# Modulation chunks in the order 0, 2, 1, 3, with z's products in halves between them

## What is computed

```python
mod   = silu(c) @ w_ada + b_ada        # sh1, sc1, g1, sh2, sc2, g2: six rows of 1024
mod_c = silu(c_ctx) @ w_ada + b_ada
u  = (rms_norm(x,   norm_pre_mix) * (1 + sc1)  + sh1)  @ w_in    # latent tokens
uc = (rms_norm(ctx, norm_pre_mix) * (1 + csc1) + csh1) @ w_in    # context tokens
# u is split: q, k, v and gate z of the delta rule, xs, B, C and gate z of the state space part,
# 48 small columns. Convolutions, two scans in both directions, w_out and a norm follow,
# then the mixture of experts: 32 experts, top 4, and the last norm
```

## Time and profile before

| | us |
|---|---|
| device time, median of 3 runs | 1446.82 |
| lowest and highest | 1443.19, 1450.98 |
| span of the profiled execution (its own device time isn't recorded apart) | 1447.1 |
| TensorE busy (matmul) in that span | 1279.4 |
| VectorE, ScalarE, GpSimd busy | 479.3, 253.1, 123.0 |
| first z product starts | 40.09 |
| last small product ends | 82.56 |

### The profile page before, as it was taken

The page is one execution under the profiler, slowest core; times in us unless marked ns, Lnnn a source line. Parts: engine busy times, 40 slices in busy tenths (PEclk is TensorE's granted clock), DMA queues, the critical chain, the costliest instruction groups (busy, mean ns, idle before and its releaser), DMA issues.

```text
span 1447.1 us, 26834 instructions
## 1 busy us (share of the span) xinstructions
PE 1279.4 (88%) x11016; PEld 586.6 (41%) x11017; DVE 479.3 (33%) x1023; ACT 253.1 (17%) x492; POOL 123.0 (8%) x168
## 2 busy tenths in 40 slices
PE   5999899447897999989898889887998999999995
PEld 1556444346665334333333333332433433433432
DVE  1236346742586423223221222121322322322323
ACT  2321523023514111111111111100100100100101
POOL 0201413443411000000000000000000000000000
PEclk9999999656798999999999999999999999999998
DMA  9506273010057799999999999999999699969993
GB/s 362 238 30 226 80 252 140 2 33 5 23 208 269 304 427 428 429 428 428 428 428 428 428 428 428 427 427 427 427 428 428 260 428 428 428 279 415 428 428 149
DMA packets 47822, 458.85 MB, mean 317 GB/s; under 512 B 4369, under 2 KB 4753, under 8 KB 22673
## 3 DMA queue, kind: packets, MB, share of 16 engines
q1 hardware_dynamic: 47762, 457.96, 76.3%
HBM read 456.31 MB, written 1.05 MB: 316 GB/s over the span
## 4 chain that ended last, share of the span: by engine, by line
PE 41%; DMA 28%; DVE 2%; ACT 1%; issue 1%; DVEq 0%; ACTq 0%
DMA arena<-in_w_up 28%; PE bank L1138 21%; PE bank L1167 8%; PE bank L1109 3%; PE bank L1100 2%; PE bank L1031 2%; PE bank L870 1%; ACT arena L1521 1%; PE bank L1131 1%; PE bank L1162 1%; ACT arena L1519 0%; PE bank L974 0%; PE bank L986 0%; PE bank L996 0%; PE bank L1042 0%
## 5 line engine op out<-in xcount | busy, mean ns | idle before, releaser
L1138 PE MATMUL bank<-arena 128*64 128x512 f32 x2176 | 483.1, 597 | 34.1 <-DMA arena<-in_w_up 19.7
L1138 PEld LDWEIGHTS bank<-arena 128*64 128x64 f32 x2176 | 154.1, 137 | 344.3 <-issue 269.6
L1167 PE MATMUL bank<-arena 128*64 128x512 f32 x1088 | 239.4, 592 | 0.0
L2179 DVE TENSOR_SCALAR arena<-bank 128x512 f32<-128x512 f32 x34 | 23.6, 693 | 390.9 <-PE bank L1138 390.9
L1167 PEld LDWEIGHTS bank<-arena 128*64 128x64 f32 x1088 | 78.2, 136 | 138.4 <-issue 136.0
L638 PE MATMUL bank<-arena 128*128 128x512 f32 (+1 forms) x320 | 122.4, 539 | 0.6 <-DMA arena<-in_wfm 0.6
L2160 DVE TENSOR_TENSOR arena<-arena,bank 128x512 f32<-128x512 f32 x140 | 86.6, 682 | 6.0 <-PE bank L1109 6.0
L638 PEld LDWEIGHTS bank<-arena 128*128 128x128 f32 x320 | 60.5, 192 | 60.5 <-issue 54.9
L1100 PEld LDWEIGHTS bank<-arena 128*128 128x128 bf16 x1680 | 60.4, 119 | 27.0 <-DVE arena L2183 25.8
L1109 PE MATMUL bank<-arena 64*128 64x512 f32 x280 | 69.6, 614 | 0.9 <-ACT arena L1523 0.9
L1100 PE MATMUL bank<-arena 128*128 128x64 bf16 x1680 | 64.2, 199 | 1.1 <-DVE arena L2101 1.1
(11 more groups left out here) (339 smaller groups left out, 1107.1 us busy)
## 6 DMA issues: line engine op xcount, KB each, us to landing
arena<-in_w_gate SPq DMA_DIRECT2D x64, 2048.0 KB, 20.1
arena<-in_w_up SPq DMA_DIRECT2D x64, 2048.0 KB, 21.7
arena<-in_w_down SPq DMA_DIRECT2D x64, 2048.0 KB, 20.3
arena<-in_w_ada SPq DMA_DIRECT2D x12, 2048.0 KB, 8.9
arena<-in_wfm SPq DMA_DIRECT2D x20, 512.0 KB, 6.6
arena<-in_wz SPq DMA_DIRECT2D x2, 2048.0 KB, 19.9
arena<-in_w_out SPq DMA_DIRECT2D x2, 2048.0 KB, 8.2
arena<-in_x SPq DMA_DIRECT2D x2, 1024.0 KB, 10.0
```

Source lines behind the costliest of these rows:

```text
L1138: last = mm(ps[m][64 * c_:64 * c_ + 64, :], xcT[:, k, :], ring[:, 2 * h_ + m, k % 4, 512 * c_:512 * c_ + 512], start=False, stop=(k == KT ...
L1167: last = mm(ps[2][64 * c_:64 * c_ + 64, :], hidT[:, k % 4, 64 * (k // 4):64 * (k // 4) + 64], ring[:, 4 + h_, k % 4, 512 * c_:512 * c_ + 5 ...
L2179: v.tensor_scalar(hid[:, 0], ps[0][:, :], LIMIT, None, ALU.min).then_inc(*L.mark("a"))
```

## The change

The weights of z come in halves of four k tiles (1 MB), each with a mark of its own. The order of the transfers is: bias (as 16 rows of 128), chunk 0, x, cols, chunk 2; when chunk 0's product is done, the first half of z's matrix 0, chunks 1 and 3; when chunk 2's product is done, the first half of matrix 1, both second halves, ctx; then as before. Chunks 1 and 3 get areas that are written later (kT and on, v_tm and on), chunk 2 the second place of `ada`.

`modc` and `a1` are formed in two halves: features 0 to 511 when the columns of chunks 0 and 2 are there, 512 to 1023 with those of chunks 1 and 3. xmT's k tiles 0 to 3 are written after the first half, ScalarE doing row tile 2 and VectorE row tile 3 (for ctx, the old split stays); GpSimd permutes in halves too. z's products over k tiles 0 to 3 stand between the chunks and those over k tiles 4 to 7 behind them, in banks that hold the sum meanwhile: 0 and 1 for matrix 0, 4 and 6 for matrix 1. A second buffer, `xh2`, holds every other row tile; the root's refining is done for two tiles at once. ScalarE takes the squares of x ahead of the copy of chunk 0.

The bias product L519 and its constant `first` are gone: the 16 bias rows are turned once by TensorE into bank 7, copied by VectorE to `badac`, and added where `modc` was copied.

The diff, cut where it only renames or repeats:

```diff
-    for name, n in (("ident", 128), ("pick", 2), ("first", 32), ("eps", 1), ("lnq", 1), ("zero", 1),
+    for name, n in (("ident", 128), ("pick", 2), ("eps", 1), ("lnq", 1), ("zero", 1),
...
+        bada, badac = area("nrm", 0, 128)[0:16], area("nrm", 128, 16)
...
+        def xh_of(t):
+            return xh2 if t % 2 else xh
...
-        bada = area("nrm", 0, 4 * 512)
+        xh2 = area("nrm", D, D)
         brow = [xin[:, 0], rows[:, 3], xin[:, 1], area("nrm", 0, D)]
-        ada_early = [area("xmT", 0, 4096), arena[:, AT["kT"][0]:AT["kT"][0] + 4096]]
+        ada_early = [arena[:, AT["kT"][0]:AT["kT"][0] + 4096], arena[:, AT["v_tm"][0]:AT["v_tm"][0] + 4096]]
+        ada_bank = (0, 3, 1, 2)
+        ada_sem = ("ada0", "ada2", "ada1", "ada3")
+        xt_bank = {2: (4, 5), 3: (6, 7), 0: (5, 7), 1: (0, 1)}
+        z_bank = ((0, 1), (4, 6))
         def ada_of(use):
-            return view(ada_early[use - 2], KT, 512) if use in (2, 3) else ada[:, use % 2]
+            return view(ada_early[use // 2], KT, 512) if use in (1, 3) else ada[:, use // 2] if use < 4 else ada[:, use % 2]
...
             def load_ada(use):
-                load(f"ada{use % 4 if use < 4 else use % 2}", ada_of(use), w_ada_v[:, :, use * 512:use * 512 + 512])
-            load("bada", bada[0:1, :], b_ada[:, 0:4 * 512])
+                load(ada_sem[use] if use < 4 else f"ada{use % 2}", ada_of(use), w_ada_v[:, :, use * 512:use * 512 + 512])
+            def load_wz(m, half):
+                load(f"wz{m}{half}", ada[:, m, 4 * half:4 * half + 4], wz[m, :, 4 * half:4 * half + 4])
+            load("bada", bada, b_ada[:, 0:2 * D].rearrange("o (i p) -> (o i) p", p=P))
             load_ada(0)
-            load_ada(1)
             load("x", xin, x.rearrange("(t p) d -> p t d", p=P))
             load("cols", area("cols"), cols)
             load_ada(2)
+            sp.wait_ge(*L.at("pe", "slot", 0))
+            load_wz(0, 0)
+            load_ada(1)
             load_ada(3)
-            for m in range(2):
-                sp.wait_ge(*L.at("pe", "slot", m))
-                load(f"ada{m}", ada[:, m], wz[m])
-                if m == 0:
-                    load("ctx", ctx_in, ctx.rearrange("(t p) d -> p t d", p=P))
+            sp.wait_ge(*L.at("pe", "slot", 2))
+            load_wz(1, 0)
+            load_wz(0, 1)
+            load_wz(1, 1)
+            load("ctx", ctx_in, ctx.rearrange("(t p) d -> p t d", p=P))
             load("const", area("const", NFIRST), consts[:, NFIRST:])
...
             def ada_chunk(use, bank):
                 if use < 4:
-                    pe.wait_ge(*L.at("in", f"ada{use}", 1))
+                    pe.wait_ge(*L.at("in", ada_sem[use], 1))
                 else:
-                    pe.wait_ge(*L.at("in", f"ada{use % 2}", use // 2 + 1))
-                if 2 <= use < 4:
-                    pe.wait_ge(*L.at("act", "mod", use - 2))
-                if use < 4:
-                    pe.wait_ge(*L.at("in", "bada", 1))
-                    mm(ps[bank][0:32, :], const("first")[0:1, :], bada[0:1, 512 * use:512 * use + 512], start=True, stop=False)
+                    pe.wait_ge(*L.at("in", f"ada{use % 2}", use // 2))
+                if use == 3:
+                    pe.wait_ge(*L.at("dve", "modc", 0))
                 for k in range(KT):
                     g = k % 4
                     last = mm(ps[bank][32 * g:32 * g + 32, :], sct[:, k, :], ada_of(use)[:, k, :],
-                              start=(k < 4 and (g > 0 or use >= 4)), stop=(k >= 4))
+                              start=k < 4, stop=(k >= 4))
                 last.then_inc(*L.mark("ada", use))
                 book.new[("pe", "slot", use)] = book.new[("pe", "ada", use)]
...
             def mod_columns(use):
                 pe.wait_ge(*L.at("act", "mod", use))
+                bank = ps[2 + use % 2]
                 for i in range(4 * use, 4 * use + 4):
-                    last = mm(ps[2][:, 2 * i:2 * i + 2], modp[:, 128 * i:128 * i + 128], const("pick"),
+                    last = mm(bank[:, 2 * i:2 * i + 2], modp[:, 128 * i:128 * i + 128], const("pick"),
                               start=True, stop=True)
-                last.then_inc(*L.mark("modc"))
-            def rows_turned(n, t):
+                last.then_inc(*L.mark("modc", use))
+            def rows_turned(t):
                 pe.wait_ge(*L.at("dve", "xh", t))
-                if n >= 2:
-                    pe.wait_ge(*L.at("act", "xmT", (2, 3, 0, 1)[n - 2]))
-                    pe.wait_ge(*L.at("dve", "xmT", (2, 3, 0, 1)[n - 2]))
+                if t == 0:
+                    pe.wait_ge(*L.at("act", "xmT", 2))
+                    pe.wait_ge(*L.at("dve", "xmT", 3))
+                if t == 1:
+                    pe.wait_ge(*L.at("act", "z", 1))
                 for k in range(KT):
-                    last = nc.tensor.transpose(ps[4 + 2 * (n % 2) + k // 4][:, (k % 4) * 128:(k % 4) * 128 + 128],
-                                               xh[:, 128 * k:128 * k + 128], ident)
+                    last = nc.tensor.transpose(ps[xt_bank[t][k // 4]][:, (k % 4) * 128:(k % 4) * 128 + 128],
+                                               xh_of(t)[:, 128 * k:128 * k + 128], ident)
                 last.then_inc(*L.mark("xT", t))
-            ada_chunk(0, 0)
-            ada_chunk(1, 1)
-            mod_columns(0)
-            ada_chunk(2, 0)
-            mod_columns(1)
-            rows_turned(0, 2)
-            rows_turned(1, 3)
-            ada_chunk(3, 1)
-            mod_columns(2)
-            mod_columns(3)
             smp = view(ps[3][:, 0:192], 4, 48)
-            def z_of(m, t):
-                pe.wait_ge(*L.at("in", f"ada{m}", 2))
+            def z_of(m, t, half):
+                pe.wait_ge(*L.at("in", f"wz{m}{half}", 1))
                 if m:
-                    pe.wait_ge(*L.at("pool", "perm"))
-                    pe.wait_ge(*L.at("act", "z", t))
+                    pe.wait_ge(*L.at("pool", "perm", half))
                 else:
-                    pe.wait_ge(*L.at("act", "xmT", 2 + t))
-                    pe.wait_ge(*L.at("dve", "xmT", 2 + t))
+                    pe.wait_ge(*L.at("dve" if t else "act", "xmT" if half else "xmTA", 2 + t))
                 base = 256 + 256 * m + 128 * t
-                for k in range(KT):
-                    last = mm(ps[t], xmT[:, k, base:base + 128], ada[:, m, k, :], start=(k == 0), stop=(k == KT - 1))
-                last.then_inc(*L.mark("zt", m, t))
-                book.new[("pe", "z", m)] = book.new[("pe", "zt", m, t)]
+                for k in range(4 * half, 4 * half + 4):
+                    last = mm(ps[z_bank[m][t]], xmT[:, k, base:base + 128], ada[:, m, k, :], start=(k == 0), stop=(k == KT - 1))
+                if half:
+                    last.then_inc(*L.mark("zt", m, t))
+                    book.new[("pe", "z", m)] = book.new[("pe", "zt", m, t)]
...
-            z_of(0, 0)
-            z_of(0, 1)
-            rows_turned(2, 0)
+            pe.wait_ge(*L.at("in", "bada", 1))
+            nc.tensor.transpose(ps[7][:, 0:16], bada, ident[0:16, 0:16]).then_inc(*L.mark("bada"))
+            ada_chunk(0, ada_bank[0])
+            mod_columns(0)
+            rows_turned(2)
+            ada_chunk(2, ada_bank[2])
+            rows_turned(3)
+            mod_columns(2)
+            z_of(0, 0, 0)
+            z_of(0, 1, 0)
+            ada_chunk(1, ada_bank[1])
+            ada_chunk(3, ada_bank[3])
+            mod_columns(1)
+            z_of(1, 0, 0)
+            mod_columns(3)
+            z_of(1, 1, 0)
+            z_of(0, 0, 1)
+            z_of(0, 1, 1)
+            rows_turned(0)
             pe.wait_ge(*L.at("in", "wsm", 1))
             small_of(2, 0, 32)
-            z_of(1, 0)
-            rows_turned(3, 1)
+            z_of(1, 0, 1)
+            rows_turned(1)
             small_of(3, 0, 32)
             pe.wait_ge(*L.at("act", "xmT", 0))
             pe.wait_ge(*L.at("dve", "xmT", 0))
             small_of(0, 0, 48)
-            z_of(1, 1)
+            z_of(1, 1, 1)
             pe.wait_ge(*L.at("act", "xmT", 1))
             pe.wait_ge(*L.at("dve", "xmT", 1))
             small_of(1, 0, 48)
...
-            def xt_out(L, f, t, n):
+            def xt_out(t, ks, step):
                 act.wait_ge(*L.at("pe", "xT", t))
-                act.wait_ge(*L.at("dve", "a1"))
+                act.wait_ge(*L.at("dve", "a1", 0 if ks[0] == 0 and t >= 2 else 1))
                 j = 0 if t >= 2 else 1
                 base = {2: 256, 3: 384, 0: 0, 1: 128}[t]
-                for k in range(KT // 2):
-                    src = ps[4 + 2 * (n % 2) + k // 4][:, (k % 4) * 128:(k % 4) * 128 + 128]
-                    f(xmT[:, k, base:base + 128], src, ACT.Identity, scale=a1[:, k, j:j + 1], bias=modc[:, k, j:j + 1]).then_inc(*L.mark("xmT", t))
+                for k in ks:
+                    src = ps[xt_bank[t][k // 4]][:, (k % 4) * 128:(k % 4) * 128 + 128]
```

(92 more changed lines are left out.)

13 lines of the change are left out of this document (5 added, 8 removed).

## The result

The changed kernel takes 1432.62 us (median of 4 runs, 1430.97 to 1434.44), the kernel before 1445.01 beside it (1441.79 to 1450.98). The ratio is 0.9912, its 95% interval 0.9887 to 0.9936: 12.7 us faster, 9.3 to 16.3. The forecast was 1438.7 with a range of 1433.5 to 1444.5. So the direction was right, the gain came out half as large again as the 8.1 us forecast, and the time lies just under the range. Over all runs of the study the median before is 1444.6 (107 runs), after 1432.4 (12 runs): 12.2 us.

A forecast was written before the change was run, and what follows sets the result against it. TensorE was taken as the bound from 40 us, with holes before while modulation weights arrive. Small products ending at 74.2 against 82.4 saved 8.1 us: 1446.8 - 8.1 = 1438.7, range 1433.5 to 1444.5.

The forecast's parts named there:

- The bound, and the holes: Until 40 us modulation weights arrive and TensorE has holes; from 40 us TensorE is the bound; work moved forward saves one for one.
- The arrivals: Landing times in the new transfer order: x 12.6, chunk 2 18.1, chunk 1 26.0, chunk 3 31.3, last z half 39.1 us.
- z's first product at 26.2: TensorE's first z product in the front was to start at 26.2 us, against 40.09 before.
- End of the front at 74.2: Small products were to end at 74.2 us against 82.4 before, saving 8.1 us.
- The base of 82.4: End of the small products in the kernel before, read from the profile, against which the new front's end was set.
- I find no event tied to absolute time: the gain is carried: Front to kernel end: the front's gain reaches the end; clock shifts behind it set at zero, ±3 us kept for the range.
- The rule against the change: TensorE's K cut in the middle: by the skill's rule each group behind a wait pays the low clock again.
- rival 3: Clock stays at 1.2 GHz from 26.2 us until both first z halves are done: slower, 1456.9 us; chance 0.03.
- Rival 1: Front as summed, but chunk 2 at high clock (1.7 more), shorter fall behind small products (1.3 more): 1435.7 us; chance 0.18.
- Rival 2: Front as summed, but a cover fails or a later stage's clock gives 3 to 4 us back: 1442.8 us; chance 0.23.
- Rival 4: Half products wait for xmT until the second modulation step, or transfers dry up at SP's wait: 1446.8 us; chance 0.04.
- the cover of 1.4 us: Second modulation step ends at 45.8 us, while TensorE asks for it at 47.2.

## Why the prediction was right in kind and short in size

The front did what was forecast, but for the clock in it. Two things the sum had wrong: it put the move of all tiles at nothing, and it was short by 2 to 3 us up to the first expert product. The time, moreover, was counted from a base that was 2.2 us high.

- **The bound, and the holes.** Right. Taken away, z's first halves leave two waits for DMA of 5.3 us; put in, there is no wait behind 27.84, and the DMA share is 0.99 to 1.04 from 10 to 55 us, as forecast.
- **The arrivals.** Right: ScalarE takes up x at 13.45 (12.6 forecast), and TensorE waits for no chunk but the first. All covers held: chunk 3 is used right behind chunk 1, and the second modulation step ends at 47.4, ahead of z's second halves at 48.6 (45.13 plus a half of 3.5).
- **z's first product at 26.2.** It came at 27.84 in the first profile, with x later, and at 27.0 to 27.1 in the others: short by 0.8 to 1.6. The turning of tile 2 alone took 1.95 to 1.97, at the low clock, where the sum had 1.04.
- **End of the front at 74.2.** 74.8, 77.3, 77.1 and 77.1: the sum took one fall of the clock at z for 1.4 us; in three of four executions it cost 3 (z's first group 9.9 to 10.0 us instead of 8.55, and the clock back at 1.00 only by 34 us and not by 32). Mean 76.6, short by 2.4.
- **The base of 82.4.** The same error on the other side: 82.4, 84.7, 85.7 and 82.6, mean 83.8. The sum was made from one execution, of the shorter sort. The two errors nearly cancel: 8.1 were forecast, the means differ by 7.3 there and by 8.1 two products of the loop later (9.1 with six executions each). This term held, or was short by 1, in part by luck.
- **"All bytes are those of before but for 16 KB of constants."** The failed term. I counted `first` as bytes of a transfer and not as a move of everything behind it, and put the expert stage at no change. The transfers of one expert went from 29.42 to 29.37 us and the stage from 972.6 to 970.9, 1.7 us (9 and 11 profiles).
- **"I find no event tied to absolute time: the gain is carried", and the clock behind the front set at zero.** Up to the first expert product the changed kernel is 10 to 11 us ahead and not 8.1. This part of the sum was 2 to 3 us short. Whether the front itself was underrated (9.1 with six executions) or the clock behind it gave the rest is open: the stretch behind the front differs by 3.0 in four pairs of profiles, by 0.9 in six, and not at all over all 20.
- Sum: 10 to 11 up to the experts and 1.7 in them are 11.7 to 12.7, against 12.2 between the medians of all runs.
- **The base, 1446.8.** This was the median of three runs; over 107 runs it is 1444.6. Of the 6.3 us between the forecast time and 1432.4, 2.2 are this and 4.1 the gain. From 1444.6 the same sum and the same spread would have given a range down to 1431.3.
- **The rule against the change.** The Trainium skill (TensorE: Matmul & The Clock Gate, section "HAM oscillation — how this bites in real kernels") warns of pauses between K tiles, behind which the clock is low again. The trace agrees for the pause of 2.3 us ahead of z, which cost 1.4 to 3 us; but the halves here fill waits and make none, and rival 3 with its 1456.9 stayed away: the clock was back by 32 to 34 us.
- **Rival 1** came nearest in time, 1435.7, and mostly not by its own means: chunk 2 took 3.28 to 3.64 us in the four profiles and not 1.93; the fall behind the small products was shorter by 0.8 (15.68 against 16.48), where it had 1.3. **Rival 2**, a gain partly given back by the clock behind, did not come. **Rival 4** and the cover of 1.4 us, 1.2 in the trace, cost nothing.
- The range had 5.2 us below the forecast, for rival 1 and scatter. An error of the base had no room in it, and a term that was not seen had none either.

## What to carry to other kernels

Work moved into a wait ahead of it is priced well from one profile, but the base must come from several executions when the clock falls in it. Look at what an edit does to the layout: removing one small constant moved all tiles and changed the rate of the experts' transfers. Where TensorE waits or runs only small products, idle products or a large product between them made 2.4 GHz likelier here; they cost what they outlast the wait by (14 of them delayed chunk 2). And before a surplus is explained by one stage of one pair of profiles, the same stage should be read in several: here it went away.
